# Sixteen GpSimd scatters of an MoE's routing lists, held until the first expert's gate and up products are done

## What is computed

```python
logits = (xf @ w_router).astype(jnp.float32) + b_router.astype(jnp.float32)
top_val, top_idx = lax.top_k(logits, TOP_K)
gates = jax.nn.softmax(top_val, axis=-1)
...
def expert_block(args):
    tok, g, e = args
    xb = xf[tok]
    hu = xb @ w_gate_up[e] + b_gate_up[e]
    a = jnp.minimum(hu[:, :D_FF], SWIGLU_LIMIT)
    lin = jnp.clip(hu[:, D_FF:], -SWIGLU_LIMIT, SWIGLU_LIMIT)
    act = a * jax.nn.sigmoid(SWIGLU_ALPHA * a) * (lin + 1)
    return (act @ w_down[e] + b_down[e]) * g[:, None].astype(xb.dtype)
```

## Time and profile of the kernel before

| | us |
|---|---|
| median of 3 runs | 1415.22 |
| lowest and highest | 1413.18, 1415.27 |
| the profiled execution, its own time | 1424.46 |
| its span (first to last instruction) | 1422.7 |
| PE busy in the span | 1322.9 (93%) |
| POOL busy in the span | 312.6 (22%) |
| DMA, mean over the span | 317 GB/s |

### The profile page before, as it was taken

How to read it: one execution, slowest core, us unless ns; L and a number is a source line. 1 busy time by engine, 2 the same in 40 slices (tenths; PEclk the granted TensorE clock), 3 DMA queues, 4 the chain that set the end, 5 groups by cost and what they waited for, 6 DMA issues and landing times.

```text
span 1422.7 us, 32891 instructions
## 1 busy us (share of the span) xinstructions
PE 1322.9 (93%) x13982; PEld 656.1 (46%) x13982; DVE 474.7 (33%) x759; ACT 206.8 (15%) x314; POOL 312.6 (22%) x267
## 2 busy tenths in 40 slices
PE   4999999987999999999999999999999999999982
PEld 4876677872444344444333333333334444443331
DVE  5555553561222222322322222222222332222332
ACT  4333332330010000100010000000001000000012
POOL 6834236124011111111111111111111111111101
PEclk9999999989999999999999999999999999999996
DMA  7512111666999999999999999999999999999964
GB/s 209 136 30 60 60 60 59 239 250 237 344 394 402 386 406 394 397 398 389 395 397 392 397 388 389 390 390 394 381 394 388 389 392 392 385 384 394 397 269 135
DMA packets 96715, 451.11 MB, mean 317 GB/s; under 512 B 14161, under 2 KB 39009, under 8 KB 47536
## 3 DMA queue, kind: packets, MB, share of 16 engines
q1 hardware_dynamic: 83280, 426.27, 76.6%
q0 software_dynamic: 10768, 19.86, 5.9%
q10 hardware_dynamic: 2640, 4.59, 0.9%
HBM read 440.01 MB, written 19.25 MB: 323 GB/s over the span
## 4 chain that ended last, share of the span: by engine, by line
PE 50%; DMA 31%; SPq 7%; DVE 5%; issue 4%; ACT 1%; POOL 1%; DVEq 0%; POOLq 0%; ACTq 0%
PE gu_bank L1431 23%; DMA raw<-in_w_gate_up_dram 19%; PE bank L1445 11%; DMA raw_b<-in_w_gate_up_dram 10%; PE bank L1210 4%; SPq L371 4%; PE bank L1212 4%; PE bank L1211 4%; SPq L375 3%; PE bank L1300 1%; DVE probs L974 1%; ACT probs L716 1%; PE bank L1264 1%; PE bank L1419 1%; DVE probs L961 1%
## 5 line engine op out<-in xcount | busy, mean ns | idle before, releaser
L1431 PE MATMUL gu_bank<-raw,xT 128*32 128x512 f32 x3072 | 344.0, 593 | 21.7 <-DMA raw<-in_w_gate_up_dram 20.3
L1431 PEld LDWEIGHTS gu_bank<-raw,xT 128*32 128x32 f32 x3072 | 100.9, 110 | 257.5 <-issue 185.3
L1125 DVE TENSOR_TENSOR gate_in<-gu_bank,b_gu 128x768 f32<-128x768 f32 x32 | 30.6, 958 | 564.9 <-PE gu_bank L1431 532.1
L1445 PE MATMUL bank<-raw_a,aT 128*32 128x256 f32 x2232 | 166.8, 380 | 0.0
L1448 PE MATMUL bank<-raw_a,aT 128*32 128x256 f32 x744 | 166.4, 380 | 0.0
L1431 PE MATMUL gu_bank<-raw_c,xT 128*32 128x512 f32 x1488 | 165.9, 592 | 0.0
L581 POOL DMA_INDIRECT sum_rows<-y_out,scatter_list x32 | 47.5, 1484 | 460.7 <-ACT y_out L830 379.7
L1445 PEld LDWEIGHTS bank<-raw_a,aT 128*32 128x32 f32 x2232 | 88.8, 110 | 62.1
L1149 DVE STREAM_TRANSPOSE aT<-lin_in 128x768 f32<-128x768 f32 x32 | 51.2, 1599 | 197.8 <-PE bank L1448 197.7
L816 ACT ACTIVATE xT<-bank 128x384 f32<-128x384 f32 x66 | 28.9, 488 | 549.4 <-PE bank L1419 539.0
L1431 PEld LDWEIGHTS gu_bank<-raw_c,xT 128*32 128x32 f32 x1488 | 53.9, 110 | 105.8 <-issue 89.9
(11 more groups left out here) (214 smaller groups left out, 1685.9 us busy)
## 6 DMA issues: line engine op xcount, KB each, us to landing
raw<-in_w_gate_up_dram SPq DMA_DIRECT2D x128, 1024.0 KB, 30.0
raw_c<-in_w_gate_up_dram SPq DMA_DIRECT2D x62, 1024.0 KB
raw_a<-in_w_down_dram SPq DMA_DIRECT2D x62, 1024.0 KB
raw_b<-in_w_gate_up_dram SPq DMA_DIRECT2D x32, 1024.0 KB
raw_b<-in_w_down_dram SPq DMA_DIRECT2D x32, 1024.0 KB
raw_e<-in_w_gate_up_dram SPq DMA_DIRECT2D x31, 1024.0 KB
raw_d<-in_w_down_dram SPq DMA_DIRECT2D x31, 1024.0 KB
raw<-in_w_in_dram SPq DMA_DIRECT2D x24, 512.0 KB, 5.3
```

What stands on the lines that cost most here:

```text
L1431: ins = pe.matmul(gu_bank[c * GROUP:(c + 1) * GROUP, r, :], xT[:, i, r * GROUP:(r + 1) * GROUP], w[:, c], start=first, stop=last)
L1445: pe.matmul(bank_[c * GROUP:(c + 1) * GROUP, cols], aT[:, k, c * GROUP:(c + 1) * GROUP], w[:, at:at + QUARTER], start=first and r % 2 == 0 ...
```

## The change

On POOL, ahead of the sixteen scatters, one more wait: until w_used has reached GU_CHUNKS = 8, that is until PE has finished the gate and up products of expert 0.

```diff
             pool.wait_ge(lists_emptied, 16)
             pool.wait_ge(entry_made, 1)
             pool.wait_ge(entry_ready, 1)
+            pool.wait_ge(w_used, GU_CHUNKS)
             for n in range(TT * TOPK):
                 pool.indirect_dma_start(out=lists, out_offset=bass.IndirectOffsetOnAxis(ap=dest[:, n:n + 1], axis=0),
                                         in_=entry[:, n, :], in_offset=None, bounds_check=last_place,
```

## The result

The changed kernel takes 1426.05 us (median of 5 runs, 1424.10 to 1429.47) against 1415.22 (five runs, 1411.82 to 1416.25). The ratio is 1.0087 with a 95% interval from 1.0067 to 1.0108: slower by 9.5 to 15.3 us. The profiled execution took 1425.52 us, with a span of 1423.8, hardly more than the 1424.46 of the profiled execution before. So the two traces show a loss of 1 us and the timed runs one of about 11. Why they differ is the main thing that the experiments had to find.

A forecast was written before the change was run, and what follows sets the result against it. PE bounds until its lead of loaded slots is used up, then the weight stream. Wait +12.4, slower first chunk +1.7, load under way -1.3 sum to +12.8: 1428.0 from 1415.2 us; range 1414.5 to 1434.

The forecast's parts named there:

- the rule that the prediction took from the windows: First expert: what happens there moves the end by the time it adds to, or takes from, the weight stream.
- First products at full rate without scatters: PE's first gate and up products: eight chunks in 20.81 us, ending at 337.8 instead of 349.45.
- Gather to turns: Expert 2's rows, from the gather's issue at 367.9 to landing at 376.9: 9.0 us, beside the weight stream.
- Lateness of the first down product: PE could begin the down products at 365.4 but waits for the gather until 377.8: +12.4 us.
- Clock: PE's first chunk after the idle wait runs in part at the lower clock level: +1.7 us.
- The load still under way: Weight ring: a load still running as the next is issued lets 1.3 us of the wait cost nothing.
- POOL's later steps: Broadcast and scatter_list load behind the gather: covered by the first down products, priced at nothing, otherwise at most 8.3 us.
- The loss of 11.7 us: PE's first products, 325 to 339 us: a loss taken as caused by recording and absent from timed runs.
- the sign of my reading: Profiled execution hardly changes (1424 to 1427) while timed runs get slower; that difference marks the loss as recorded only.
- Rival A: The loss is real in timed runs and moves to the second products beside the wait; 1415.5, 1414 to 1418; chance 0.30.
- Rival B: Real loss, smaller in the second products, and gather landing in 5.3 us; faster, end near 1411.0; chance 0.06.
- Rival C: Scatters' small packets queue behind the weight loads, the last landing 19.2 us later; end at 1447; chance 0.08.

The follow-up runs named there:

- e1: The kernel before, unchanged, traced a second time; ratio 0.9995 (0.9981 to 1.0008).
- e7: Changed kernel with expert 2's rows gathered ahead of the held scatters, using expert 1's list (result not the reference's); ratio to the kernel before 1.0006.
- e4: Kernel before with eight scatters issued at once and only the other eight held until the eighth chunk; ratio 1.0033, median 1418.94 us.
- e2: Changed kernel with the scatters held until the fourth chunk instead of the eighth; ratio to the kernel before 1.0024, median 1417.67 us.
- e3: Changed kernel with the scatters held until the sixth chunk instead of the eighth; ratio to the kernel before 1.0069, median 1424.89 us.
- e8: Kernel before with scatters in their old place and only expert 2's list load held until w_used reaches 16; ratio 1.0080.
- e5: Changed kernel with the scatters held for twelve chunks instead of eight; ratio to the kernel before 1.0145, median 1433.34 us.
- e9: The kernel before, unchanged, on a chip where it takes 1425.28 us (17 runs); this run took 1423.76 us.
- e10: The kernel before, unchanged, once more on the chip where it takes 1425.28 us; this run took 1423.71 us.
- e11: Scatters held for one chunk only (w_used at 1), against the kernel before on the chip where that takes 1425.28 us; ratio 1.0000.

## Why the prediction was right

The first down products of each trace, counted from its first gate product, beside the timed ratios:

| kernel | first down product, us | against e1 | ratio to before | in us |
|---|---|---|---|---|
| e1, as before | 48.15 | 0 | 0.9995 | -0.7 |
| e7, rows early | 47.99 | -0.2 | 1.0006 | +0.8 |
| e4, half held | 51.41 | +3.3 | 1.0033 | +4.7 |
| e2, hold 4 | 52.66 | +4.5 | 1.0024 | +3.4 |
| e3, hold 6 | 57.51 | +9.4 | 1.0069 | +9.8 |
| the change | 58.87 | +10.7 | 1.0087 | +12.3 |
| e8, list held | 59.81 | +11.7 | 1.0080 | +11.3 |
| e5, hold 12 | 68.50 | +20.4 | 1.0145 | +20.5 |

The last column agrees with the third within the intervals, some 2 to 3 us wide on each side. This bears out the rule that the prediction took from the windows: what PE loses at the first expert, the weight stream loses, and the end with it.

Point by point:

- First products at full rate without scatters, 20.8 us: 20.74. Right. They have it beside the scatters too, in e1 and e8, on two chips.
- Scatters 0.3 us behind PE, the sixteenth 19.18 us later: 0.92 us behind (340.48 against 339.56, the modelled end of the last product) and 19.58.
- Scatters to list load 3.79 us: 4.96. List load to gather 5.87: 5.82. Right within 1.2 us.
- Gather to turns 9.0 us: 4.37. This was the mis-sized term. I had taken the value under the stream, and e2 with 9.25 shows that it is right there; but this gather is issued when PE has waited for 5.9 us, the ring is full and the stream quiet (DMA share 0.31 from the gather to the turns).
- Lateness of the first down product, 12.4 us: 10.7 against e1.
- Clock, 1.7 us: 2.1. Of these 0.6 are already in the start of the down products, for the slower turns. The other 1.5 follow in the down products, whose first seven groups of four records take 2.99 us where e1 has 1.54.
- The load still under way, 1.3 us in favour: no run tests this term by itself.
- Sum, +12.8: with the terms as measured 10.7 + 1.5 - 1.3 = 10.9; the result is +10.8 by the medians, +12.3 by the ratio, which has 9.5 to 15.3.
- POOL's later steps are free: in e7, where the broadcast is late as well (58.1 us after the first gate product, 40.7 in e1), nothing is lost.
- That the profiled execution would hardly change (1424 to 1427) while the timed runs get slower: 1425.52.

One step was right in its outcome and wrong in its reason. "The loss of 11.7 us looks like something that recording causes": e1 was recorded and has no loss, and on the chip of e9 all timed runs carry it. What I had from the two times, that the timed kernel before lacks the loss, was true; it lacked it most likely because it ran on other chips. The sign of the forecast rested on this step, so in that much it was luck. With the timed runs on a chip like that of e9, a recorded and a timed run would have agreed, and the loss would have had to be counted as real. That the profiled executions hardly differ while the timed runs do, which was to be the sign of my reading, came true too and doesn't tell recording from chip.

The Trainium skill (NOTIFIC — the notification-queue block, 7.1 Overflow: three behaviours, one of which stalls the engine) says that the pipeline that writes trace records holds up its producers rather than lose a record inside the block. No run here bears out that this happened. SP's waits that end in a "remote" release, as in the earlier trace rows, are in the four traces with the loss (before, e9, e10, e11) and in none of the ten without it, so they belong to what slows PE there; what it is stays open. Nor is "in just this stretch" exact: six scatters of the earlier trace rows start before the slow stretch of the earlier trace rows, beside matmuls at the full rate.

Rival A, no change where the loss is real, is then a statement about chips like that of e9. It wasn't tried: the changed kernel never ran on such a chip. By the terms it would come out nearly even there: down products at 58.2 to 58.9 us in the changed kernel, at 60.6 in e9. That supposes that the scatters don't slow the second products there. e11, where the loss moved with the scatters, makes it likelier that they do; then the second products would end some 11.3 us later, at about 59 instead of 47.3 us, beside the wait and not on top of it, and the down products would begin near 60, an estimate from e1, e9 and e11. Either way it is argued from the traces and not shown. Rival B's quick landing did happen (4.37 us), but without a loss to give back it only made the cost smaller. Rival C didn't: the list was complete 4.96 us after the last scatter, in the middle of the stream.

None of the held versions beats the kernel before, and the runs don't point to one that could: in e1 POOL asks for expert 2's rows at 348.35, and PE turns them at 366.19 without a wait. The line behind them, from the view of x_got, is the time from this gather's issue to its landing:

```profile
342.98 0.60 POOL L558 DMA_DIRECT2D gather_list<-lists  x1 [5.07 <-DMA lists<-entry,dest]
348.35 1.00 POOL L571 DMA_INDIRECT x_got<-xn_rows,gather_list  x1 [4.77 <-issue]
```

```profile
DMA to landing us min/median/max: 6.8/6.8/6.8
```

The rows are there 11 us early. A hold has less than that to use, since later steps can take longer: e2's scatters begin 12.5 us later than e1's (counted from the first gate product), and PE waits 4.22 us, which leaves 8.3; and with the 9.25 us of e2 in place of 6.8, e1's rows would be 8.6 us early. The lists have slack, and all that a hold can do is use it up.

## What to carry to other kernels

Before holding back a transfer, follow all that stands behind it in its queue to the engine that bounds the kernel, and count its slack: here the rows could be held back by some 8 us, and every hold that goes beyond this makes PE wait. A gap in one trace is a gain only if the timed runs have it; when the profiled execution and the median lie further apart than the runs scatter, take a second trace before pricing the gap, and see whether both ran on the same chip. Don't add up durations of transfers that were taken beside a full weight stream if the wait itself makes the stream pause.

## What the runs showed of the hardware that was not expected

- Chips differ by as much as this change costs: 1414 against 1425 us for the same kernel, nearly all of it (11.3 us) in one stretch of 13 us, in which PE does 28 matmul records instead of some 120 while POOL issues scatters of 16-byte entries, at a granted clock of 1.00 and a DMA share of 0.27. On that chip the stretch moved with the scatters (e9, e11), and on two others the same scatters beside the same matmuls cost nothing (e1, e8). What holds PE there is open; no run on that chip left the scatters out or moved them behind the first products.
- A gather of 96 rows of 4 KB reached PE sooner the less the weight stream ran beside it: 9.25 us after its issue at a DMA share of 1.01 (e2), 7.31 at 0.76 (e3), 4.37 at 0.31 (the change), 4.15 at 0.26 (e5).
- A list load that depends on scatters started 1.43 us after the last of them with the stream paused (e5) or nearly so (DMA share 0.02 in e9 and e11), and 3.87 to 5.29 us after it beside the stream (e1 to e4, the change).
